# Expert 0's high parts and first rows in the routing block, two activation tables loaded ahead, and the sample tile on both column halves of TensorE

## What is computed

```python
m = (silu(c) @ w_mod + b_mod)            # shift, scale and gate rows, one set per sequence
h = x * (1 + sc1) + sh1
z = h @ w_in                             # 1024 x 2072: pool | sgu u | sgu v | q | kv (3 branches) | gates
mix = concat(pool_mix, sgu_mix, attention)
x = layer_norm(ALPHA * x + (1 + g1) * (mix @ w_out))
h2 = x * (1 + sc2) + sh2
s = sigmoid(h2 @ router_w)               # 16 experts in 4 groups, top 2 of the best group
# tokens sorted by expert, padded to blocks of 128 rows
y = (silu(x_blk @ w_gate[e]) * (x_blk @ w_up[e])) @ w_down[e]
x = layer_norm(ALPHA * x + (1 + g2) * sum_k w_k * y_k)
```

## Time and profile before

| | us |
|---|---|
| median of 3 runs | 1401.73 (1397.19 to 1402.51) |
| the profiled execution | 1402.17 |
| its span, first to last instruction | 1400.2 |
| TensorE busy, matmul | 1241.0 (89%) |
| VectorE busy | 722.3 (52%) |
| ScalarE busy | 542.6 (39%) |
| GpSimd busy | 112.0 (8%) |

### The profile page before, as it was taken

How to read it: one execution, slowest core, us unless ns; L and a number is a source line. 1 busy time by engine, 2 the same in 40 slices (tenths; PEclk the granted TensorE clock), 3 DMA queues, 4 the chain that set the end, 5 groups by cost and what they waited for, 6 DMA issues and landing times. The chain is left out here.

```text
span 1400.2 us, 21334 instructions
## 1 busy us (share of the span) xinstructions
PE 1241.0 (89%) x7878; PEld 904.1 (65%) x7879; DVE 722.3 (52%) x1452; ACT 542.6 (39%) x910; POOL 112.0 (8%) x167
## 2 busy tenths in 40 slices
PE   3899999999578999999979994499999999999771
PEld 1466667665366666666658883477888887888630
DVE  0212222221335466566756766878556588575148
ACT  0110000000134577565552221567545567554132
POOL 1001011000000000000000000111001011010050
PEclk9799999999677899999999996799999999999886
DMA  9933355000547040000023324799769679794472
GB/s 327 325 143 130 142 205 89 20 12 12 140 127 275 1 121 1 1 2 1 2 85 136 118 101 157 256 374 357 267 238 353 240 251 390 259 365 138 178 293 97
DMA packets 89697, 235.57 MB, mean 168 GB/s; under 512 B 7450, under 2 KB 15061, under 8 KB 89463
## 3 DMA queue, kind: packets, MB, share of 16 engines
q1 hardware_dynamic: 76711, 192.19, 39.8%
q0 software_dynamic: 8144, 27.62, 5.5%
q10 hardware_dynamic: 4768, 14.75, 2.8%
HBM read 196.49 MB, written 40.13 MB: 169 GB/s over the span
## 5 line engine op out<-in xcount | busy, mean ns | idle before, releaser
L2194 PE MATMUL psum<-w_hi,x_parts 128*128 128x512 f32 x736 | 239.9, 398 | 9.1 <-DVE x_parts L2313 9.0
L2306 DVE TENSOR_TENSOR w_lo<-raw,w_hi 128x2048 fp32r<-128x2048 f32 x96 | 215.5, 2286 | 57.3 <-ACT w_hi L2253 57.2
L2253 ACT CAST w_hi<-raw 128x2048 fp32r<-128x2048 f32 x96 | 178.6, 1913 | 82.8 <-DVE work L2324 51.4
L596 PE MATMUL psum<-low,high 128*128 128x512 f32 (+5 forms) x576 | 198.9, 499 | 1.7 <-ACT high L718 1.7
L2194 PEld LDWEIGHTS psum<-w_hi,x_parts 128*128 128x128 f32 x736 | 139.5, 190 | 40.9 <-issue 11.9
L596 PEld LDWEIGHTS psum<-low,high 128*128 128x128 f32 (+1 forms) x576 | 104.8, 187 | 78.8 <-issue 68.1
L2194 PE MATMUL psum<-w_lo,x_parts 128*128 128x512 f32 x368 | 144.4, 392 | 0.0
L1502 DVE CUSTOM_DVE_ANT_0 low<-psum,high 128x512 f32<-128x512 f32 (+5 forms) x172 | 93.0, 579 | 77.7 <-PE psum L1203 66.5
L2194 PE MATMUL psum<-w_hi,a_parts 128*128 x368 | 121.4, 401 | 5.9 <-DVE a_parts L2319 5.9
L1415 ACT ACTIVATE low<-low,high 128x640 f32<-128x640 f32 (+9 forms) x140 | 98.8, 708 | 44.0 <-DVE high L1502 43.8
L1233 PE MATMUL psum<-keep,low 128*128 128x128 f32 (+1 forms) x556 | 103.8, 294 | 11.4 <-ACT high L1426 4.8
(11 more groups left out here) (317 smaller groups left out, 1434.7 us busy)
## 6 DMA issues: line engine op xcount, KB each, us to landing
raw<-in_moe_w_gate SPq DMA_DIRECT2D x16, 2048.0 KB, 11.0
raw<-in_moe_w_up SPq DMA_DIRECT2D x16, 2048.0 KB
raw<-in_moe_w_down SPq DMA_DIRECT2D x16, 2048.0 KB, 10.8
high<-in_w_mod SPq DMA_DIRECT2D x12, 2048.0 KB, 13.8
y_d<-work ACTq DMA_DIRECT2D x24, 512.0 KB, 6.8
high<-in_x_prompt SPq DMA_DIRECT2D x16, 512.0 KB, 4.3
y_d<-high SPq DMA_DIRECT2D x1, 8192.0 KB, 23.5
low<-in_w_in SPq DMA_DIRECT2D x3, 2048.0 KB, 15.1
```

The lines of the kernel that those rows point to most:

```text
L596: mm = pe.matmul(c.bank(2 + n % 2)[0:T, 0:w], hT[i % 2][:, k, 0:T], c.w_in[:, k, a:a + w], start=(k == 0), stop=(k == KT - 1))
L2194: mm = pe.matmul(out, left[l][:, k * P:(k + 1) * P], w[:, bass.ds(at + k * step, 512)], start=n == 0, stop=n == len(steps) - 1)
L2253: act.copy(c.w_hi[:, at:at + PART // 2], c.raw[:, o:o + PART // 2]).then_inc(hi_done[p], 1)
L2306: dve.tensor_tensor(c.w_lo[:, at:at + PART // 2], c.raw[:, o:o + PART // 2], c.w_hi[:, at:at + PART // 2].bitcast(F32), ALU.subtract).then ...
```

## The change

Five things change:

1. **Projection.** For tile 8 each chunk is made in two column parts, the first on partitions 0 to 63 and the second on partitions 64 to 127 of the same bank, by alternating products. The copies read from both places.
2. **Output.** Tile 8's product is made of plain float32 products, `mix` by `w_out`, its two width halves on the two partition halves of bank 0; no high and low parts are made for it. `g1s` takes the place of `g1` and is loaded after VectorE has read `g1` for the last prompt tile. `squares` moves so that `w_out` stays whole.
3. **Tables.** ScalarE does one Sigmoid of one element at the end of the output block, and one Silu of one element behind the sigmoid of routing.
4. **Routing.** ScalarE makes the high parts of expert 0's three matrices in the routing block, and GpSimd fetches the first block's rows there as soon as `ids_i` stands.
5. **Experts.** ScalarE begins with `x_part(0)`. TensorE does twelve filling transposes ahead of `turn_x(0)` instead of behind it. `w_hi` and `work` are laid out from the routing block on.

```diff
+SAMPLE_HALVES = (256, 128, 256, 128)
@@ chunk
+                cut = SAMPLE_HALVES[n] if i == smp else w
+                parts = [(0, a, cut)] + ([(NS, a + cut, w - cut)] if cut < w else [])
                 for k in range(KT):
-                    mm = pe.matmul(c.bank(2 + n % 2)[0:T, 0:w], hT[i % 2][:, k, 0:T], c.w_in[:, k, a:a + w],
-                                   start=(k == 0), stop=(k == KT - 1))
+                    for lo, at, wide in parts:
+                        mm = pe.matmul(c.bank(2 + n % 2)[lo:lo + T, 0:wide], hT[i % 2][:, k, 0:T], c.w_in[:, k, at:at + wide],
+                                       start=(k == 0), stop=(k == KT - 1))
@@ block_output, sync
-            for v, dst in ((2, g1s), (4, scale2s), (3, shift2s)):
+            for v, dst in ((4, scale2s), (3, shift2s)):
                 sp.dma_start(dst[0:NS, :], sample_rows(c, v)).then_inc(vec2_in, 16)
             for i in range(NT):
                 T = tile_rows(i)
+                if i == smp - 1:
+                    sp.wait_ge(o_ev, smp)
+                    sp.dma_start(g1s[0:NS, :], sample_rows(c, 2)).then_inc(vec2_in, 16)
@@ block_output, project
                     for n in range(2):
+                        if i == smp:
+                            mm = pe.matmul(c.bank(0)[NS * n:NS * n + NS, :], c.mix[:, k, SEQ:], c.w_out[:, k, n * 512:(n + 1) * 512],
+                                           start=(k == 0), stop=(k == KT - 1))
+                            continue
@@ block_output, scalar
-                if i + 2 < NT:
+                if i + 2 < smp:
                     high_parts(i + 2)
+            act.activation(squares[0:1, 0:1], eps[0:1, :], ACT.Sigmoid)
@@ block_routing
         @block.scalar
         def _(act):
             act.activation(s, c.logits, ACT.Sigmoid).then_inc(sg, 1)
+            act.wait_ge(sg, 1)
+            act.activation(c.misc[:, 272:273], s[:, 0, 0:1], ACT.Silu)
+            for p in range(3):
+                act.wait_ge(c.raw_in[p], 16)
+                for h in range(2):
+                    at = PART * p + h * PART // 2
+                    act.copy(c.w_hi[:, at:at + PART // 2], c.raw[:, at:at + PART // 2]).then_inc(c.hi_done[p], 1)
+
+        @block.gpsimd
+        def _(pool):
+            pool.wait_ge(tab_ready, 2)
+            first_rows(c, pool)
@@ block_experts, tensor
-            turn_x(0)
             for f in range(4):
                 mm = pe.transpose(c.bank(6)[:, f * P:(f + 1) * P], c.ident, c.ident)
             mm.then_inc(a_ps, 1)
             for f in range(8):
                 mm = pe.transpose(c.bank(2 + f // 4)[:, f % 4 * P:(f % 4 + 1) * P], c.ident, c.ident)
             mm.then_inc(down_done, 1)
+            turn_x(0)
@@ block_experts, scalar and vector
-            expert_loop(act, slot, split)
+            expert_loop(act, lambda: x_part(0), slot, split)
...
+            def first():
+                split(0, 0, 0, None)
+                x_part(0)
+                split(1, 0, 0, None)
+                split(2, 0, 0, None)
...
-            expert_loop(dve, slot, split)
+            expert_loop(dve, first, slot, split)
```

More of the change, by code:

```diff
@@ L734, in _ @@
                 act.copy(zp[i % 3][0:T, :], c.bank(2)[0:T, 0:PW])
-                act.copy(zuv[s][0:T, 0, :], c.bank(2)[0:T, PW:2 * PW]).then_inc(z_act, 1)
+                act.copy(zuv[s][0:T, 0, :], c.bank(2)[NS:P, 0:PW] if i == smp else c.bank(2)[0:T, PW:2 * PW]).then_inc(z_act, 1)
                 if i == 0:
@@ L1687, in block_output @@
     g1, scale2, shift2, lng, lnb, t0, *t2 = (c.view(o + D * n, D) for n in range(8))
-    g1s, scale2s, shift2s = (c.view(L_ + D * n, D) for n in range(3))
+    g1s = g1
+    scale2s, shift2s = (c.view(L_ + D * n, D) for n in (1, 2))
     st = c.view(o + 8 * D, 24)
-    squares = c.view(W_, D)
+    squares = c.view(L_, D)
     assert o + 8 * D + 24 <= MIX_
@@ L1746, in project @@
                         pe.wait_ge(o_ev, i - 1)
-                    pe.wait_ge(mix_lo, i + 1)
+                    if i < smp:
+                        pe.wait_ge(mix_lo, i + 1)
                 for k in range(first, first + 4):
@@ L1951, in block_routing @@
                          "keys_in", "consts_in"))
+    c.hi_done = [sem(f"hi_done{p}") for p in range(3)]
+    c.id_set, c.fetches, c.xb_in = sem("id_set"), sem("fetches"), sem("xb_in")
     with nc.Block() as block:
@@ L2092, in load_expert, with first_rows @@
         sp.dma_start(dst, src).then_inc(c.raw_in[p], 16)
+def first_rows(c, pool):
+    pool.tensor_copy(c.id_now[:, :], c.ids_i[:, 0:1]).then_inc(c.id_set, 1)
+    pool.wait_ge(c.id_set, 1)
+    pool.sem_inc(c.fetches, 1)
+    pool.indirect_dma_start(c.work[:, 0:D], None, c.h2_d, bass.IndirectOffsetOnAxis(ap=c.id_now[:, 0:1], axis=0)).then_inc(c.xb_in, 16)
 def block_experts(c):
@@ L2106, in block_experts @@
     aT = [c.a_parts[:, DE * i:DE * (i + 1)] for i in range(2)]
[L2107 to L2110 removed]
+    (x_ps, x_hi, x_lo, gate_done, up_done, down_done, sil, a_ready, a_ps, a_hi, a_lo, y_act, y_dve, y_out) = (
+        sem(n) for n in ("x8_ps", "x8_hi", "x8_lo", "gate8_done", "up8_done", "down8_done", "silu8", "a_ready",
+                         "a_ps", "a_hi", "a_lo", "y_act", "y_dve", "y_out"))
+    xb_in, id_set, fetches = c.xb_in, c.id_set, c.fetches
     c.v_in, c.x1_in = sem("v9_in"), [sem(f"x9_in{i}") for i in range(NT)]
[L2112 removed]
+    hi_done = c.hi_done
     used = (gate_done, up_done, down_done)
@@ L2120, in place, with expert_loop @@
         return PART * (p + (e_odd if p == 2 else 0))
-    def expert_loop(eng, slot, split):
+    def expert_loop(eng, first, slot, split):
         def nothing(p):
@@ L2140, in section @@
                 slot(end - 1, lambda p: split(p, e + 1, 1 - odd, end))
-        for p in range(3):
-            split(p, 0, 0, None)
-            if p == 0:
-                slot(None, None)
+        first()
         with eng.Fori(0, NE // 2 - 1) as pair:
@@ L2168, in _, with fetch @@
         def _(pool):
-            def fetch(s, first):
-                ins = pool.tensor_copy(c.id_now[:, :], c.ids_i[:, 0:1] if first else c.ids_i[:, bass.ds(s, 1)])
+            def fetch(s):
+                ins = pool.tensor_copy(c.id_now[:, :], c.ids_i[:, bass.ds(s, 1)])
                 ins.then_inc(id_set, 1)
@@ L2248, in split @@
                 act.wait_ge(c.raw_in[p], e * 16 + 16)
-                if begun is not None and p < 2:
+                if p < 2:
                     act.wait_ge(used[p], begun)
```

64 lines of the change are left out of this document (33 added, 31 removed).

## The result

The changed kernel took **1380.71 us** (median of 4 runs, 1379.26 to 1386.32), the kernel before on the same chip 1399.62 us (4 runs): ratio 0.9871, 95% interval 0.9834 to 0.9909, which is 18.1 us faster (the two medians lie 18.9 us apart). Run again in two later sets, with their own runs of before, the changed kernel took 1382.75 and 1383.0 us, ratios 0.9899 (0.9876 to 0.9922) and 0.9897 (0.9872 to 0.9921): 14.1 and 14.4 us. The three sets give 18.1, 14.1 and 14.4 us, all above the 13.0 of the sum; but 13.0 us is a ratio of 0.991, which lies at the edge of the first interval and inside the other two, so the times alone do not exclude it.

A forecast was written before the change was run, and what follows sets the result against it. Most stages were taken to follow TensorE, each block lasting as long as its slowest engine. Projection -10.1, output -3.9 and experts +1.0 gave -13.0 us, from a median of 1401.73 to 1388.7; range 1383 to 1393.5.

The forecast's parts named there:

- the 13.0 of the sum: Whole kernel: projection -10.1, output block -3.9 and experts' start +1.0 us make -13.0 us.
- Part 1, projection: Projection's sample tile: paired column halves shorten the four chunks, -10.1 us, range 8.5 to 10.6 less.
- Part 2, output: Output block's sample tile: paired plain float32 products replace high and low parts, -3.9 us, range 3.0 to 4.1 less.
- Part 3, routing: Routing block: becomes 3.1 us longer, bound by the down load and its conversions; Sigmoid's table load is hidden.
- ScalarE ends at 887.0 and the barrier opens at about 887.65: End of routing: down weights land at 883.3, two conversions take 3.7 us, and the barrier waits for them instead of opening at 884.6.
- landed 4.2 us later, ahead of the barrier: Routing block: GpSimd's fetch of the first rows, issued at 882, lands before the barrier opens.
- the barrier does not wait for the down weights: Rival, 20%: at routing's end the barrier opens at 883.3 and the experts gain 3.2 us; kernel at 1384.5.
- Part 4, experts: Experts' start: first product -0.2 us, at 895.0; second block's product about 1 us later, +1.0, bounds -1.5 to +4.
- that stays: Experts: the second product's 1.0 us delay lasts, since queues are full until 985 and TensorE has no gaps from there.
- the last of the sum, +1.0: Experts' start: the second block's product moves from 910.78 to about 911.8 because its gate load is issued later, +1.0 us.
- little net change: Rival, 6%: long column halves in projection and output pair at only 0.75 of serial time; kernel at 1396.6.
- the slower case: Rival, 4%: column halves run one after the other, the projection gains nothing and output loses; 1405.4 to 1408.4.

The follow-up runs named there:

- up_low_first: Changed kernel with the first rows' fetch and down's conversions back in the experts block, and VectorE making up's low parts before the rows'; 1385.88 us, ratio 0.9907.

## Why the prediction was wrong in size and right in direction

**Part 1, projection: right.** The chunks came at 3.62, 1.97, 3.62 and 2.29 us (about 3.6, 1.9, 3.6 and 2.2 forecast), 10.2 us less; alone the part measured 9.4. ScalarE's and VectorE's extra copies lay in idle time as said, and the tail stayed. The condition behind it, which the prediction took from the queries without stating it, is the alternation: 6.26 us without it.

**Part 2, output: right.** 3.5 us by the profile, 4.6 alone, 3.9 forecast. The cap that I set (VectorE busy with tile 7, at most 4.05 us) was nearly reached, but did not decide: TensorE's product still ends last, 0.38 us behind VectorE.

**Part 3, routing: the length about right by luck, the reason wrong.** The step "ScalarE ends at 887.0 and the barrier opens at about 887.65", 3.1 us longer, failed on its cause. The block became 2.3 us longer because its end waits for GpSimd's fetch, and the fetch was costed at nothing: "landed 4.2 us later, ahead of the barrier". By my own numbers it was 886.2, 0.8 us ahead of ScalarE, and since the down load landed sooner than the row of before had it (issued 1.96 us behind the block's start instead of 3.5; ScalarE's last conversion ended at 23.9 us, not 25.9) the order turned round. The length came near only because the fetch and the conversions end within 1.3 us of each other. The rival "the barrier does not wait for the down weights" was half true in its condition: the load did land sooner and the conversions did not hold the barrier, but they still ended 2.1 us behind VectorE, and the barrier did not open at 883.3 (22.2 us behind the start of routing).

**Part 4, experts: the sizes at the start right, "that stays" wrong.** The first product came 33.1 to 34.3 us behind the start of routing (34 forecast), the second 50.8 to 51.6 (50.6 forecast). Then this delay was gone by expert 6: I had read full queues as a reason why a delay lasts, and a delay of 1 us did not. What took it back stays open. The loads of up for expert 1 were issued sooner (36.7 to 37.4 us behind the start of routing in the changed kernel against 38.2 to 38.4) and those of gate 0.4 to 0.7 us later, but in `up_low_first` up's stands at 31.6 us without any gain, so an earlier load of up alone does not explain it.

**The term that failed** is thus the last of the sum, +1.0, in whose place stand -1.9 us by the profiles (-1.7 timed). About 0.8 of the 2.9 us between them is the Silu loads of the loop, which the prediction counted as one load with nothing behind it; the rest would be the forecast delay that did not last and the Sigmoid load, which I had as hidden. How these two share the rest the runs do not tell: their effects are of the size of the differences between two profiles of one kernel.

**What is left of the miss.** Forecast and first measurement are 8.0 us apart. The basis was 3.1 us too high (1401.73 against 1398.6); the terms give 15.7 us instead of 13.0, 2.7 us; the remaining 2.2 us is the first set of runs, whose kernel was measured 2.0 to 2.3 us slower on the next two occasions. This split is arithmetic on medians whose intervals are as wide as its pieces; that the last term had the wrong sign is what the runs bear out best. With the sum unchanged and the better basis the forecast would have been 1385.6.

**The profiled pair exaggerates.** Its spans are 20.2 us apart, of which the change explains about 16. The projection ahead of the sample tile gave 3.84 us without any edit, the combination 2.9; the untouched stretch from the start of compression to the start of the output block gave back 4.1 (357.5 us in before, 361.6 after, 355.7 to 363.4 in the others).

The other rivals of the prediction: the chunks overlap at 256 columns as at 128, which ends "little net change", and the slower case, halves one after the other, needed an order of issue that the diff doesn't have.

## What to carry to other kernels

Float32 products on the two halves of the array's columns overlap only if they alternate in issue order; split a tile of 64 rows that way and cap the gain by the engine that reads the result. Before adding work to a block, list what its end waits for on every engine, transfers that GpSimd issued among them, and count every table load in the loop, not the first. Where full queues set the pace, do not price a shift of a microsecond in full (here it was gone 90 us on, while one of 3.3 us lasted), and take the basis from more than three runs, or forecast the ratio.

## What the hardware showed that was not expected

- Neighbouring float32 instructions with 64 rows on the same column half take 196 ns each for 256 columns, on alternating halves 113 ns, in one piece (512 columns) 440 ns.
- The end of a block comes 0.4 us behind the landing of GpSimd's indexed fetch, 4.5 to 4.8 us behind its issue, also where no engine in the block waits for its data. Whether a load that SyncE issues holds it too was not tried.
- ScalarE loads Silu's table ten times in a loop of 23 blocks, 1.28 us each, unless one Silu stands ahead of the loop. The Trainium skill ("ScalarE: Activation LUTs", What ACT_TABLE_LOAD costs) adds a drain of 1380 ns to the load of 1283 ns; here the load starts directly behind the conversion before it and the activation 10 ns behind the load (1050.04 + 1.28 to 1051.33), and no such drain shows.
